# Two channel tiles of the gated convolution computed in token tiles and transposed back, in a four-layer float32 block on one core

## The chip, the core and the metric

The kernel runs on one NeuronCore of a Trainium2 chip. The engines are TensorE (PE: matmuls; its weight loads are PEld), VectorE (DVE), ScalarE (ACT), GpSimd (POOL) and the DMA queue that SyncE (SP) issues. The metric is the device time of one execution in microseconds (us), as the median of the runs shown.

## The reference, cut to what matters

A sequence of 512 tokens with 1024 channels passes four layers, each of them a mixer, a layer norm, a SwiGLU feed-forward and a layer norm. The change lies at the opening of the third layer's mixer:

```python
def short_gated_conv(p_a, conv_w):          # p_a = [B gate | C gate | value], 512 channels each
    return b_gate * causal_dwconv(c_gate * val, conv_w)      # 3 taps along the tokens

def multiscale_pool(u, w_grp, scale):       # u: 512 channels in 4 groups, windows 2, 4, 8, 16
    pooled = trailing_mean(u, window) - u   # along the tokens, each channel by itself
    return einsum("bsgc,gcd->bsgd", pooled, w_grp) * scale

def even_mixer(x, w_in, conv_w, pool_w, pool_scale, w_out):
    p = x @ w_in                            # 1024 -> b, c, v, u of 512 channels each
    return concat([short_gated_conv(b, c, v), multiscale_pool(u)]) @ w_out
```

In front of it stand the second layer's feed-forward (`ffn1`) and its layer norm.

## The kernel before, in words

Every float32 product is made of three matmuls: the weight is split into `whi` (its rounded high part) and `wlo` (the rest), the activation likewise (`XH`, `XL`), and hi·hi, hi·lo and lo·hi are summed in a PSUM bank. Weights come in units, 128x2048 values or so, into a ring of three places (`raw`, `whi`, `wlo`). For each unit in turn SP loads `raw`, ACT writes `whi` (`split_w`, L447), POOL writes `wlo` (`split_w`, L788) and PE uses it: `begin_unit` (L909) waits for `lo_ready`, that is for POOL, and the first matmul of a unit hands the unit before it back (`w_used`), upon which ACT may overwrite its place. ACT and POOL do all their work in one fixed order, written out by hand, so that a split of weights can stand behind a split of activations and the other way round.

**Layouts.** A channel tile is 128 channels x 512 tokens in one bank: the weight is stationary and all 512 tokens move through, so its first matmul needs all tokens. A token tile is 128 tokens x 512 channels: the tokens are stationary, and each of the four token tiles needs only its own tokens.

**The seam in question.** The feed-forward ends with token tiles t = 0 to 3 (`last_units`). DVE normalises tile t (`token_norm`) while PE computes t+1; PE transposes the normalised tile (`token_transposes`, eight 128x128 transposes), ACT copies it to `XH` and DVE writes `XL`. The last tile is transposed when its norm is done. Into the third layer PE then goes with `opening(2)` (L953): the first two channel tiles of u, which need all 512 tokens. Into the second layer it goes with `early_units` (L1112) instead: two units as four token tiles of 512 columns; the parts for t = 0 and 1 stand before the transposes of t = 3, those for t = 2 and 3 behind them.

**The third mixer's order.** The six units `ev_in` 0 to 5 hold two channel tiles each: u0 u1, u2 u3, then c and v of channel tile 0, 1, 2, 3. Behind them PE computes the four pooling products (`ev_pool`, from `EPH` and `EPL`) and four tiles of b. DVE works through four pooling tiles (copy of u, 1 to 4 doubling adds, the mean, two 16-column edge operations: L1953 to L1963, result `EP`) and then four convolution tiles (copy of c, product with v, three taps: L1614, L1968 to L1973, result `EY`). ACT's order is: the `whi` of `ev_in` 1 to 4, the four `EPH`, the `whi` of `ev_in` 5, `ev_pool`, `ev_b` 0 and 1. POOL's order is the same with `wlo` and `EPL`. (`ev_in` 0 has been split within the feed-forward.)

Of the kernel before, what the change touches and what calls it, by code (L numbers as in the profile page):

```python
# [26 lines left out]
F32 = mybir.dt.float32  # L27
F32R = mybir.dt.float32r
ALU = mybir.AluOpType
ACT = mybir.ActivationFunctionType  # L30

P = 128
S = 512
NB = S // P
D = 1024
KD = D // P
# [5 lines left out]
HALF = 512  # L42
# [123 lines left out]
def build(nc, x, xT, par, con, rcon, gb, w, out):  # L166
    ctx = ExitStack()
    with ctx:
        def sb(name, shape, dt=F32, stack=ctx):
            return stack.enter_context(nc.sbuf_tensor(name, shape, dt))  # L170

        def sem(name):
            return ctx.enter_context(nc.semaphore(name))
# [19 lines left out]
        idle = ExitStack()  # L193
# [4 lines left out]
        idle = ExitStack()  # L198
        fPT1 = sb("fPT1", [P, NB, S], F32, idle)
        idle.close()  # L200
        idle = ExitStack()
        mPT1 = sb("mPT1", [P, NB, S], F32, idle)
        idle.close()
        idle = ExitStack()
# [16 lines left out]
        ident = cons[:, CCOL["ident"]:CCOL["ident"] + P]  # L221
# [58 lines left out]
        EY = sb("EY", [P, KD, S], F32, ph)  # L280
        ec = shift
        EP = sb("EP", [P, 4, S], F32, ph)
        EPH = sb("EPH", [P, 4, S], F32R, ph)
        EPL = sb("EPL", [P, 4, S], F32R, ph)
        EAH = sb("EAH", [P, 4, S], F32R, ph)
        EAL = sb("EAL", [P, 4, S], F32R, ph)
        ez = sb("ez", [P, 2 + S], F32, ph)
# [20 lines left out]
        idle = ExitStack()  # L308
# [75 lines left out]
        gt_done = sem("gt_done")  # L384
        gt_free = sem("gt_free")
        cum_ready = sem("cum_ready")
        mem_ready = sem("mem_ready")
        small_dve = sem("small_dve")
        small_act = sem("small_act")
# [54 lines left out]
        def _(act):  # L444
            unit, tiles, srcs, auxf, gates, small = (Count() for _ in range(6))

            def split_w(n=1):  # L447

                for _ in range(n):
                    name, i, size, off, overlaps = UNITS[unit.n]  # L450
                    arrivals = unit.n // SEMS + (1 if unit.n % SEMS else 0)
                    act.wait_ge(raw_ready[unit.n % SEMS], 16 * arrivals)
                    if overlaps >= 0:
                        act.wait_ge(w_used, overlaps + 1)
                    act.copy(whi[:, off:off + size], raw[:, off:off + size]).then_inc(hi_ready, 1)  # L455
                    unit.add()
# [16 lines left out]
            def layer_norm(banks, early):  # L473

                for t in range(NB):
                    if t == 3 and early:
                        split_w()
                    for d in range(2):
                        act.wait_ge(xt_done, halves.at(1))
                        act.copy(XH[:, 4 * d:4 * d + 4, t * P:(t + 1) * P],  # L480
                                 bank[banks[(2 * t + d) % 4]][:].rearrange("p (k q) -> p k q", q=P)).then_inc(xh_ready, 1)
                        halves.add()
# [154 lines left out]
            split_w(2)  # L637
            layer_norm((0, 1, 2, 3), True)
            ffn()
            layer_norm((4, 5, 6, 7), False)  # L640


            split_w(4)
            for j in range(4):
                split_x(EPH[:, j, :], EP[:, j, :])
            tiles.add(12)
# [138 lines left out]
        def _(pool):  # L785
            unit, his, whis = Count(), Count(), Count()

            def split_w(n=1):  # L788

                for _ in range(n):  # L790
                    name, i, size, off, overlaps = UNITS[unit.n]
                    pool.wait_ge(hi_ready, whis.at(1))
                    pool.tensor_tensor(wlo[:, off:off + size], raw[:, off:off + size],  # L793
                                       whi[:, off:off + size].bitcast(F32), ALU.subtract).then_inc(lo_ready, 1)
                    unit.add()
                    whis.add()
# [21 lines left out]
            def layer_norm():  # L818

                for t in range(NB):  # L820
                    norms.add()
                    pool.wait_ge(tvar_ready, norms.at())
                    pool.tensor_tensor(troot[:, t:t + 1], tvar[:, t:t + 1], neg_half[:, 0:1], ALU.pow).then_inc(troot_ready, 1)  # L823
# [49 lines left out]
            layer_norm()  # L873
            ffn()
            layer_norm()
            split_w(4)
            for j in range(4):
                split_x(EPL[:, j, :], EP[:, j, :], EPH[:, j, :])
# [25 lines left out]
        def _(pe):  # L904
# [42 lines left out]
            def unit_tiles(nt, b0):  # L947

                off = begin_unit()
                for t in range(nt):  # L950
                    tile((b0 + t) % 4, [off + (k * nt + t) * P for k in range(KD)])

            def opening(nt, ks=range(KD)):  # L953

                off = begin_unit() - ks[0] * nt * P

                def lhs(wt, k, t):
                    return wt[:, off + (k * nt + t) * P:off + (k * nt + t + 1) * P]

                for k in ks:  # L960
                    if k % 4 == 0:
                        pe.wait_ge(xh_ready, norms.at(k // 4 - 1))
                    for which in (whi, wlo):
                        for t in range(nt):
                            if k == 0 and which is whi:
                                claim(t)
                            release(pe.matmul(bank[t][:], lhs(which, k, t), XH[:, k, :], start=k == 0 and which is whi, stop=False))  # L967
                for k in ks:
                    if k % 4 == 0:
                        pe.wait_ge(xl_ready, norms.at(k // 4 - 1))  # L970
                    for t in range(nt):
                        ins = pe.matmul(bank[t][:], lhs(whi, k, t), XL[:, k, :], start=False, stop=k == KD - 1)
                        if k == KD - 1:
                            tile_end(ins, t)
# [243 lines left out]
            def ffn(values=False):  # L1218
                for half in range(2):
                    n, first = HID[half], 0 if half else 2  # L1220
                    for j in range(first, n):
                        unit_tiles(2, 2 * (j % 2))
                        if half == 0 and j == 2:
                            early_transposes()
                    if first:
                        pe.wait_ge(early_lo, earlies.at())
                    ends = list(itertools.accumulate(DOWN[half], initial=0))
                    groups = [range(a, b) for a, b in zip(ends, ends[1:])]
                    for ks in groups:
                        first_steps(begin_unit(), ks, hidden, ks[0], n, 4, first)  # L1230
                    los.add(n - first)
                    tb0[0] = 4
                    last_units(groups, hidden, n, 0, half == 1, values)
# [208 lines left out]

            out_pair(OUT_KS, headed, (squares_of_head, spread_of_head, lambda: diff_out(7)))
            los.add(KD)
            ffn()


            opening(2)
            unit_tiles(2, 2)
            for i in range(4):  # L1450
                unit_tiles(2, 2 * (i % 2))
            off = begin_unit()
            for i in range(4):
                pe.wait_ge(act_lo, los.at(i + 1))
# [135 lines left out]
        def _(dve):  # L1590
# [4 lines left out]
            def link(ins):  # L1595

                ins.then_inc(step, 1)
                steps.add()
                dve.wait_ge(step, steps.at())
# [347 lines left out]
            def conv_col(k, i):  # L1947
                return pcol("conv_w", 4 * k + i)

            for i in range(4):  # L1950
                if i:
                    dve.wait_ge(src_ready, pooled + i)
                take(lambda: dve.tensor_copy(eu[0][:, PADW:], bank[i][:]))  # L1953
                dve.wait_ge(tile_free, tiles.at())
                src = eu[0]
                for d in range(i + 1):
                    dst = eu[1 + d % 2]
                    link(dve.tensor_tensor(dst[:, PADW:], src[:, PADW:], src[:, PADW - 2 ** d:PADW - 2 ** d + S], ALU.add))
                    src = dst

                link(dve.scalar_tensor_tensor(EP[:, i, PADW:], src[:, 2 * PADW:], 1.0 / WINDOWS[i], eu[0][:, 2 * PADW:], ALU.mult, ALU.subtract))
                link(dve.tensor_tensor(EP[:, i, 0:PADW], src[:, PADW:2 * PADW], cons[:, CCOL["invcnt"] + 16 * i:CCOL["invcnt"] + 16 * i + 16], ALU.mult))
                dve.tensor_tensor(EP[:, i, 0:PADW], EP[:, i, 0:PADW], eu[0][:, PADW:2 * PADW], ALU.subtract).then_inc(src_ready, 1)  # L1963
            for i in range(4):
                b = 2 * i % 4
                copy_tile(ec[:], b)
                dve.wait_ge(tile_free, tiles.at())
                take(lambda: dve.tensor_tensor(ez[:, 2:2 + S], bank[b + 1][:], ec[:], ALU.mult))  # L1968
                dve.wait_ge(tile_free, tiles.at())
                y = EY[:, i, :]  # L1970
                link(dve.tensor_scalar(y, ez[:, 0:S], conv_col(0, i), None, ALU.mult))
                for k in (1, 2):
                    link(dve.scalar_tensor_tensor(y, ez[:, k:k + S], conv_col(k, i), y, ALU.mult, ALU.add))  # L1973
            los.add(4)
            for i in range(4):
                take(lambda: dve.tensor_scalar(EY[:, 4 + i, :], bank[i][:], pcol("pool_s", i), None, ALU.mult))
# [136 lines left out]
def host_layout(inp):  # L2113
# [17 lines left out]
    w = {}  # L2131
# [30 lines left out]
    u, b = (win[:, :, i].reshape(KD, P, 2, 2, P).transpose(2, 1, 0, 3, 4).reshape(2, P, 2048) for i in (3, 0))  # L2162
    cv = win[:, :, 1:3].transpose(3, 1, 0, 2, 4).reshape(4, P, 2048)
    pool = f(inp["ev_pool_w_2"])[0].transpose(1, 0, 2).reshape(P, 512)
    w["ev_in"] = np.concatenate([u, cv])
    w["ev_pool"], w["ev_b"] = pool[None], b
    m = f(inp["ev_w_out_2"])[0]
    w["ev_o"] = down(np.concatenate([m[D // 2:], m[:D // 2]]), (4, 4))
# [62 lines left out]
```

## Time and profile before

| | us |
|---|---|
| median of 3 runs | 2356.08 (2351.93 to 2356.32) |
| the profiled execution | 2355.84 |
| its span, first to last instruction | 2354.1 |
| mean granted TensorE clock | 0.991 of full speed |

Busy shares of the span: PE 97%, PEld 78%, POOL 44%, DVE 31%, ACT 30%. The span is some 1.7 us shorter than the execution's own time. Times of instructions are counted from the span's start. A bracket behind a row of the timeline tells how long the engine sat idle before it and what released it.

### The profile page before, as it was taken

How to read it: one execution, taken by the hardware profiler on the slowest of the kernel's cores; microseconds unless marked ns; L12 is line 12 of the kernel's file. 1: busy time of each engine (PE TensorE's matmuls, PEld its weight loads, DVE VectorE, ACT ScalarE, POOL GpSimd, SP SyncE). 2: the span in 40 equal slices, each digit the busy share in tenths (PEclk: the TensorE clock that was granted, in tenths of full speed). 3: DMA queues.
4: the chain of work that ended last, by engine and by line, in shares of the span. 5: the costliest groups of instructions: out<-in, count | busy, mean ns of one | idle time of the engine just before them, and what ended most of it. 6: DMA issues, size and time to landing. Idle time of an engine off the chain costs nothing.

```text
span 2354.1 us, 24657 instructions
## 1 busy us (share of the span) xinstructions
PE 2294.1 (97%) x10303; PEld 1840.5 (78%) x10303; DVE 721.4 (31%) x1373; ACT 706.0 (30%) x1001; POOL 1026.6 (44%) x351
## 2 busy tenths in 40 slices
PE   8999999999999999999999999999998999999998
PEld 6667888888776778888878888888876667888887
DVE  6535000004466440010066410000269535000003
ACT  2453321222343232222222232222252563322220
POOL 3124553554333345445445455445532224554543
PEclk9999999999999999999999999999999999999999
DMA  4213223222212132322232232322221112332221
GB/s 169 73 72 140 93 90 107 90 75 81 99 50 90 36 125 90 107 90 83 99 110 90 90 125 90 107 90 90 99 72 36 56 53 91 124 99 98 90 90 54
DMA packets 32366, 212.60 MB, mean 90 GB/s; under 512 B 3584, under 2 KB 4736, under 8 KB 8832
## 3 DMA queue, kind: packets, MB, share of 16 engines
q1 hardware_dynamic: 32256, 211.03, 25.8%
q8 instruction: 82, 1.34, 0.2%
q14 instruction: 28, 0.23, 0.0%
HBM read 208.92 MB, written 2.10 MB: 90 GB/s over the span
## 4 chain that ended last, share of the span: by engine, by line
PE 88%; DVE 8%; ACT 2%; issue 1%; POOL 0%; DMA 0%; SPq 0%; DVEq 0%; ACTq 0%
PE bank L936 16%; PE bank L938 16%; PE bank L937 16%; PE bank L986 9%; PE bank L988 9%; PE bank L987 9%; DVE bank L2003 3%; PE bank L1047 2%; PE bank L1122 2%; PE bank L1123 2%; PE bank L1127 2%; PE bank L1165 1%; PE bank L1420 1%; PE bank L967 1%; PE bank L1025 1%
## 5 line engine op out<-in xcount | busy, mean ns | idle before, releaser
L793 POOL TENSOR_TENSOR wlo<-raw,whi 128x2048 fp32r<-128x2048 f32 (+5 forms) x184 | 842.8, 4582 | 670.7 <-ACT whi L455 662.4
L936 PE MATMUL bank<-XH,whi 128*128 128x512 f32 x1752 | 692.8, 395 | 9.3 <-POOL wlo L849 6.0
L938 PE MATMUL bank<-XH,wlo 128*128 128x512 f32 x1752 | 684.7, 391 | 0.0
L937 PE MATMUL bank<-XL,whi 128*128 128x512 f32 x1752 | 684.3, 391 | 0.0
L455 ACT CAST whi<-raw 128x2048 fp32r<-128x2048 f32 (+5 forms) x184 | 349.5, 1900 | 418.0 <-PE bank L986 304.5
L936 PEld LDWEIGHTS bank<-XH,whi 128*128 128x128 f32 x1752 | 330.4, 189 | 94.6 <-issue 19.0
L938 PEld LDWEIGHTS bank<-XH,wlo 128*128 128x128 f32 x1752 | 330.3, 189 | 70.0
L937 PEld LDWEIGHTS bank<-XL,whi 128*128 128x128 f32 x1752 | 330.6, 189 | 66.4
L1702 DVE TENSOR_TENSOR hf<-sil,bank 128x512 f32<-128x512 f32 x80 | 55.0, 688 | 814.4 <-PE bank L938 814.4
L986 PE MATMUL bank<-whi,HH 128*128 128x512 f32 x704 | 274.4, 390 | 0.0
L988 PE MATMUL bank<-wlo,HH 128*128 128x512 f32 x704 | 274.0, 389 | 0.0
L987 PE MATMUL bank<-whi,HL 128*128 128x512 f32 x704 | 273.9, 389 | 0.0
L807 POOL TENSOR_TENSOR HL<-hf,HH 128x512 fp32r<-128x512 f32 x80 | 103.6, 1295 | 376.3 <-ACT HH L503 376.3
L503 ACT CAST HH<-hf 128x512 fp32r<-128x512 f32 x80 | 49.6, 620 | 453.1 <-DVE hf L1702 453.1
L988 PEld LDWEIGHTS bank<-wlo,HH 128*128 128x128 f32 x704 | 132.1, 188 | 27.5
L987 PEld LDWEIGHTS bank<-whi,HL 128*128 128x128 f32 x704 | 132.2, 188 | 27.4
L986 PEld LDWEIGHTS bank<-whi,HH 128*128 128x128 f32 x704 | 132.1, 188 | 27.1
L1642 DVE SCALAR_TENSOR_TENSOR X<-X,bank 128x512 f32<-128x512 f32 x64 | 43.9, 687 | 279.4 <-PE bank L988 278.9
L499 ACT ACTIVATE sil<-bank 128x512 f32<-128x512 f32 x80 | 47.9, 598 | 186.2 <-PE bank L938 186.2
L823 POOL TENSOR_TENSOR troot<-tvar,neg_half 128x1 f32<-128x1 f32 x32 | 25.3, 791 | 129.8 <-DVE tvar L1668 129.8
L480 ACT CAST XH<-bank 128x512 fp32r<-128x512 f32 x56 | 30.7, 589 | 156.0 <-PE bank L1165 155.7
L2003 DVE SCALAR_TENSOR_TENSOR bank<-fz,parm,bank 128x512 f32<-128x512 f32 x90 | 68.0, 755 | 3.1
(273 smaller groups left out, 2254.1 us busy)
## 6 DMA issues: line engine op xcount, KB each, us to landing
raw<-w_ffn_gu SPq DMA_DIRECT2D x88, 1024.0 KB, 4.8
raw<-w_ffn_dn SPq DMA_DIRECT2D x40, 1024.0 KB, 4.8
GB<-gb SPq DMA_DIRECT2D x8, 1024.0 KB, 6.8
raw<-w_diff_in SPq DMA_DIRECT2D x6, 1280.0 KB, 5.7
raw<-w_ev_in SPq DMA_DIRECT2D x6, 1024.0 KB, 4.9
raw<-w_od_in SPq DMA_DIRECT2D x4, 1536.0 KB, 6.4
raw<-w_mla_pair SPq DMA_DIRECT2D x4, 1088.0 KB, 5.8
raw<-w_mla_o SPq DMA_DIRECT2D x4, 1024.0 KB, 6.0
```

Of the source, the lines that this page charges most:

```text
L455: act.copy(whi[:, off:off + size], raw[:, off:off + size]).then_inc(hi_ready, 1)
L503: act.copy(HH[:, j, :], hf[i][:]).then_inc(act_hi, 1)
L793: pool.tensor_tensor(wlo[:, off:off + size], raw[:, off:off + size], whi[:, off:off + size].bitcast(F32), ALU.subtract).then_inc(lo_ready, 1)
L807: pool.tensor_tensor(dst, src, hi.bitcast(F32), ALU.subtract).then_inc(act_lo, 1)
L936: release(pe.matmul(out, whi[:, off:off + P], xh, start=start, stop=False))
L937: pe.matmul(out, whi[:, off:off + P], xl, start=False, stop=False)
L938: return pe.matmul(out, wlo[:, off:off + P], xh, start=False, stop=stop)
L986: release(pe.matmul(bank[b][:], xh[:, rows], whi[:, off:off + HALF], start=start, stop=False))
L987: pe.matmul(bank[b][:], xl[:, rows], whi[:, off:off + HALF], start=False, stop=False)
L988: ins = pe.matmul(bank[b][:], xh[:, rows], wlo[:, off:off + HALF], start=False, stop=stop)
L1702: take(lambda: dve.tensor_tensor(hf[i][:], sil[i][:], bank[2 * i + 1][:], ALU.mult), 2)
L2003: ins = dve.scalar_tensor_tensor(acc, fz[i][:, k:k + S], wk, acc, ALU.mult, ALU.add)
```

## The change

The two first units of the mixer become c and v of channel tiles 0 and 1 (256 columns of c, 256 of v), computed as four token tiles by `early_units(0)`. ACT copies c of each token tile to SBUF (`ect`), DVE multiplies it with v from the bank (`ezt`). Then comes the unit of u0 and u1; between the two PE transposes `ezt` back into two banks of 128 channels x 512 tokens (eight 128x128 transposes), and DVE copies these to `ez` for the taps. After them come u2 u3, c and v of tile 2, c and v of tile 3. Within the last feed-forward's norm ACT splits `ev_in` 1 before the copies of the last token tile. POOL gets a wait for the whole norm before it splits `ev_in` 1. DVE's order becomes pooling 0, convolution 0, pooling 1, convolution 1, pooling 2, pooling 3, convolution 2, convolution 3. ACT and POOL keep all four `EPH` and `EPL` between `ev_in` 4 and `ev_in` 5.

```diff
@@ buffers (they lie over EAH, which is written later)
+        ect = sb("ect", [P, NB, 2 * P], F32, idle)
+        ezt = sb("ezt", [P, NB, 2 * P], F32, idle)
@@ ACT
-            layer_norm((4, 5, 6, 7), False)
-            split_w(4)
+            layer_norm((4, 5, 6, 7), True)
+            split_w()
+            for t in range(NB):
+                act.wait_ge(tile_done, tiles.at(t + 1))
+                act.copy(ect[:, t, :], bank[t][:, 0:2 * P]).then_inc(ec_ready, 1)
+            split_w(2)
             for j in range(4):
                 split_x(EPH[:, j, :], EP[:, j, :])
@@ POOL
             layer_norm()
+            pool.wait_ge(xn_ready, 2 * norms.n)
             split_w(4)
@@ PE
-            ffn()
-            opening(2)
+            ffn(True)
+            off = begin_unit()
+            tile(0, [off + 2 * k * P for k in range(KD)])
+            pe.wait_ge(tile_free, tiles.at(-1))
+            for e in range(2):
+                claim(4 + e)
+                for t in range(NB):
+                    ins = pe.transpose(bank[4 + e][:, t * P:(t + 1) * P], ezt[:, t, e * P:(e + 1) * P], ident)
+                ins.then_inc(zt_done, 1)
+                freed[4 + e] = (zt_free, e + 1)
+            tile(1, [off + (2 * k + 1) * P for k in range(KD)])
             unit_tiles(2, 2)
-            for i in range(4):
-                unit_tiles(2, 2 * (i % 2))
+            unit_tiles(2, 0)
+            unit_tiles(2, 2)
@@ DVE
+            for t in range(NB):
+                dve.wait_ge(ec_ready, t + 1)
+                take(lambda: dve.tensor_tensor(ezt[:, t, :], bank[t][:, 2 * P:4 * P], ect[:, t, :], ALU.mult))
             for i in range(4):
+                pool_tile(i)
+                if i < 2:
+                    dve.wait_ge(zt_done, i + 1)
+                    dve.tensor_copy(ez[:, 2:2 + S], bank[4 + i][:]).then_inc(zt_free, 1)
+                    dve.wait_ge(zt_free, i + 1)
+                    conv_tile(i)
+            for i in (2, 3):
                 (copy of c, product with v, conv_tile(i), as before)
@@ host
-    w["ev_in"] = np.concatenate([u, cv])
+    early = win[:, :, 1:3, 0:2].reshape(2, 4, P, HALF).transpose(0, 2, 1, 3).reshape(2, P, 2048)
+    w["ev_in"] = np.concatenate([early, u, cv[2:]])
```

## Rows read from the trace of the kernel before

**Rows 1.** The page's part 1: busy time of TensorE and its share of the span.

```profile
PE 2294.1 (97%) x10303; PEld 1840.5 (78%) x10303; DVE 721.4 (31%) x1373; ACT 706.0 (30%) x1001; POOL 1026.6 (44%) x351
```

**Rows 2.** Waits between 1195 and 1400 us: engine, line waited for, total, times, longest.

```profile
PE bank L1165 <- DVE X L1681: 3.0, 1, 3.0
...
PE bank L936 <- DVE EY L1976: 1.1, 1, 1.1
```

**Rows 3.** Timeline of PE at the seam: start, duration, instruction, idle time before it.

```profile
1208.16 1.04 PE L1165 MATMUL bank<-cons,X 128*128 128x128 f32 x8
1212.25 1.32 PE L1165 MATMUL bank<-cons,X 128*128 128x128 f32 x8 [3.05 <-DVE X L1681]
1213.78 1.19 PE L967 MATMUL bank<-XH,whi 128*128 128x512 f32 x2 [0.21 <-ACT XH L480]
```

**Rows 4.** Stretches: length, busy (count) by engine, granted clock; behind the stall, and second layer.

```profile
1213.78:1217.26 3.48, 3.48 (x9) 2.76 (x10) 1.55 (x7) 3.04 (x3) 0.65 (x1) 0.51 0.00 0
...
575.80:599.37 23.57, 23.57 (x113) 19.72 (x112) 9.65 (x17) 6.38 (x7) 10.21 (x3) 1.00 0.32 112
```

**Rows 5.** Timeline of PE: first matmuls of `ev_in` 2 and `ev_in` 5.

```profile
1237.23 0.39 PE L936 MATMUL bank<-XH,whi 128*128 128x512 f32 x1
...
1269.87 0.39 PE L936 MATMUL bank<-XH,whi 128*128 128x512 f32 x1
```

**Rows 6.** The chain that ended last: one set of eight transposes, early in feed-forward one.

```profile
246.66 0.87 PE bank L1148 x8
```

**Rows 7.** One line's instructions: DVE products of 128x256 from a bank, min/median/max ns.

```profile
L1694 DVE TENSOR_TENSOR hft<-silt,bank x16: 420/422/422, 228.8 to 2009.4; 128x256 f32<-128x256 f32 x16
```

**Rows 8.** Second layer's seam: POOL's second split there, and DVE's last token tile copy.

```profile
585.57 4.60 POOL L793 TENSOR_TENSOR wlo<-raw,whi 128x2048 fp32r<-128x2048 f32 x1 [0.53 <-ACT whi L455]
...
599.41 0.69 DVE L1614 COPY dVS<-bank 128x512 f32<-128x512 f32 x1 [2.03 <-PE bank L1127]
```

**Rows 9.** Timeline of DVE through the pooling and convolution tiles.

```profile
1226.32 0.69 DVE L1953 COPY eu<-bank 128x512 f32<-128x512 f32 x1 [10.99 <-PE bank L972]
...
1228.91 0.69 DVE L1953 COPY eu<-bank 128x512 f32<-128x512 f32 x1
1229.63 5.07 DVE L1958 TENSOR_TENSOR eu<-eu 128x512 f32<-128x512 f32 x2
...
1236.59 2.15 DVE L1958 TENSOR_TENSOR eu<-eu 128x512 f32<-128x512 f32 x3
...
1240.62 9.36 DVE L1958 TENSOR_TENSOR eu<-eu 128x512 f32<-128x512 f32 x4
...
1250.94 0.18 DVE L1963 TENSOR_TENSOR EP<-EP,eu 128x16 f32<-128x16 f32 x1
...
1252.48 0.95 DVE L1971 TENSOR_SCALAR EY<-ez,parm 128x512 f32<-128x512 f32 x1
...
1270.14 0.69 DVE L1968 TENSOR_TENSOR ez<-bank,shift 128x512 f32<-128x512 f32 x1 [4.75 <-PE bank L938]
...
1271.39 1.54 DVE L1973 SCALAR_TENSOR_TENSOR EY<-ez,parm,EY 128x512 f32<-128x512 f32 x2
```

**Rows 10.** Timeline of ACT: the `whi` of `ev_in` 5, behind the last `EPH`.

```profile
1251.67 1.91 ACT L455 CAST whi<-raw 128x2048 fp32r<-128x2048 f32 x1
```

**Rows 11.** Timeline of POOL: `wlo` of `ev_in` 3, three `EPL`, and `wlo` of `ev_in` 5.

```profile
1228.82 4.60 POOL L793 TENSOR_TENSOR wlo<-raw,whi 128x2048 fp32r<-128x2048 f32 x1 [3.04 <-ACT whi L455]
...
1244.30 5.14 POOL L807 TENSOR_TENSOR EPL<-EP,EPH 128x512 fp32r<-128x512 f32 x3
...
1251.85 1.30 POOL L807 TENSOR_TENSOR EPL<-EP,EPH 128x512 fp32r<-128x512 f32 x1 [2.41 <-ACT EPH L461]
1253.66 5.01 POOL L793 TENSOR_TENSOR wlo<-raw,whi 128x2048 fp32r<-128x2048 f32 x1 [0.52 <-ACT whi L455]
```

**Rows 12.** PE behind its longest wait, in the fourth layer: timeline rows.

```profile
1825.30 0.80 PE L1552 MATMUL bank<-fK,fQ 64*128 64x128 f32 x4 [8.31 <-DVE fK L1614]
...
1826.79 0.78 PE L936 MATMUL bank<-XH,whi 128*128 128x512 f32 x1
```

**Rows 13.** The same place as stretches (columns as in rows 4).

```profile
1830.00:1831.00 1.00, 1.00 (x4) 0.81 (x3) 0.93 (x2) 0.00 (x0) 0.00 (x0) 0.50 0.00 0
1831.00:1832.00 1.00, 1.00 (x4) 0.79 (x4) 0.00 (x0) 0.00 (x0) 0.00 (x0) 0.72 0.00 0
```

More of the change, by code:

```diff
@@ L284, in build @@
         EPL = sb("EPL", [P, 4, S], F32R, ph)
+        idle = ExitStack()
+        ect = sb("ect", [P, NB, 2 * P], F32, idle)
+        ezt = sb("ezt", [P, NB, 2 * P], F32, idle)
+        idle.close()
         EAH = sb("EAH", [P, 4, S], F32R, ph)
@@ L386, in build @@
         cum_ready = sem("cum_ready")
+        ec_ready = sem("ec_ready")
+        zt_done = sem("zt_done")
+        zt_free = sem("zt_free")
         mem_ready = sem("mem_ready")
@@ L1948, in conv_col, with pool_tile @@
                 return pcol("conv_w", 4 * k + i)
-            for i in range(4):
+            def pool_tile(i):
                 if i:
@@ L1963, in _, with conv_tile @@
                 dve.tensor_tensor(EP[:, i, 0:PADW], EP[:, i, 0:PADW], eu[0][:, PADW:2 * PADW], ALU.subtract).then_inc(src_ready, 1)
-            for i in range(4):
+            def conv_tile(i):
+                y = EY[:, i, :]
+                link(dve.tensor_scalar(y, ez[:, 0:S], conv_col(0, i), None, ALU.mult))
+                for k in (1, 2):
+                    link(dve.scalar_tensor_tensor(y, ez[:, k:k + S], conv_col(k, i), y, ALU.mult, ALU.add))
+            for t in range(NB):
+                dve.wait_ge(ec_ready, t + 1)
+                take(lambda: dve.tensor_tensor(ezt[:, t, :], bank[t][:, 2 * P:4 * P], ect[:, t, :], ALU.mult))
+            for i in range(4):
+                pool_tile(i)
[5 more added lines that the diff above has]
+            for i in (2, 3):
                 b = 2 * i % 4
@@ L1969, in _ @@
                 dve.wait_ge(tile_free, tiles.at())
[L1970 to L1973, printed above, removed]
+                conv_tile(i)
             los.add(4)
```

## The prediction

> **What bounds the kernel now.** I read the page first: PE is busy for 97% of the span [rows 1], so nearly every microsecond that PE does not stand still counts, and the work of DVE, ACT and POOL counts only where PE waits for it. Next I read the waits around the third mixer: PE waits there 3.0 us for the last token tile's norm and 1.1 us for a bank that DVE frees late [rows 2]. Then the timeline of PE at the seam. The reader should see three things: the transposes of token tile 2 at 1208.16, an idle time of 3.05 us before those of tile 3, and `opening` only from 1213.78 on, beginning slowly [rows 3]. The stretch behind it shows why: 3.48 us at a granted clock of 0.51, the lower of the two levels, 1.2 GHz instead of 2.4 [rows 4], after PE had stood still. Last I read DVE, ACT and POOL through the mixer, since the change puts their work into another order [rows 9 to 11].
>
> **Part 1: the seam itself, a gain.** From the transposes of tile 2 (1208.16) to the first matmul of the third unit, `ev_in` 2 (1237.23), PE now takes 29.07 us [rows 3, 5] for two sets of eight transposes and two units. The same work in the form that the change gives it stands in the trace already, at the second layer's seam: 23.57 us at full clock with no idle time [rows 4]. Gain: 29.07 - 23.57 = 5.50 us, made of the wait, the wait for `XH`, and the matmuls at half clock. The third mixer's units have the same size as those there, and the same number of instructions. So PE reaches `ev_in` 2 at 1208.16 + 23.57 = 1231.73.
>
> **Part 2: what is added on PE.** Eight transposes of `ezt`, 0.87 us for such a set [rows 6]. Their wait: the last product of DVE ends at about 1232.6 (in the second layer DVE gets the last token tile 0.04 us after PE has gone on [rows 4, 8]; here ACT's copy of 128x256 comes first, some 0.4 us by DVE's row for the same size, and then DVE's 0.42 us [rows 7]). PE asks for it only after tile u0, 5.44 us later (half a unit; `ev_in` 2, 3 and 4 take 1269.87 - 1237.23 = 32.64 us, 10.88 us each [rows 5]). Cost of the wait: nothing; u0 covers it, with 4.5 us to spare.
>
> Next, the splits at the seam. POOL's new wait for the norm puts `ev_in` 1 where the second layer's seam has it, and that seam runs without a gap [rows 4]; its second split there starts 9.77 us behind 575.80 [rows 8], so `wlo` of `ev_in` 2 ends at 1208.16 + 9.77 + 4.60 = 1222.5, against a use at 1231.73. Cost: nothing. But the `whi` of `ev_in` 3 and 4 now stand behind ACT's four copies of c, the last of which can't be made before 1231.8. With 1.91 us for `whi` [rows 10] and 4.60 us for `wlo` [rows 11], POOL writes `ev_in` 3 from 1234.0 to 1238.6, and `ev_in` 4 to 1243.6. PE wants them at 1231.73 + 10.88 + 0.87 = 1243.5 and 1254.4. Cost: nothing, with 4.9 us to spare at the nearer one.
>
> If nothing else happened, PE would reach `ev_in` 5 at 1254.37 + 10.88 = 1265.24, 4.63 us before the present 1269.87 [rows 5]. That is all that the change can gain.
>
> **Part 3: the split of `ev_in` 5, a loss.** PE's wait at `begin_unit` is for POOL's `wlo` of `ev_in` 5. In POOL's order it stands behind all four `EPL`, and in ACT's its `whi` stands behind all four `EPH`; both wait for DVE's fourth pooling tile. Today that tile is ready at 1251.12 and the `wlo` at 1253.66 + 5.01 = 1258.67, 7.55 us later [rows 9, 11], which leaves 11.2 us before its use at 1269.87 [rows 5]. In the new order u comes a unit and more later on PE, the use comes earlier, and DVE puts two convolution tiles between the pooling tiles.
>
> DVE's own work, uncontended: pooling tile 0 takes 1228.91 - 1226.32 = 2.59 us, each further add 0.72 us (2.15 us for three), so the four take 2.59 + 3.31 + 4.03 + 4.75 = 14.68 us; a convolution tile with its copy from the bank takes 1271.39 + 1.54 - 1270.14 = 2.79 us, two of them 5.58 us [rows 9]. It starts when u0 is complete, 1231.73 + 5.44 = 1237.2, and would end at 1257.5. The last pooling tile can't start before u3 is complete at 1254.37, so the least is 1254.4 + 4.75 = 1259.1.
>
> DVE is not uncontended. While POOL splits from 1228.82 for 4.60 us, two adds that should take 1.44 us take 5.07 us, and four adds beside a split and three `EPL` take 9.36 us in place of 2.9 [rows 9, 11]: an operation of DVE with both inputs in SBUF stands still until POOL's instruction ends, while its copies from a bank go on. In the new order POOL's splits of `ev_in` 3 and 4 (1234.0 to 1243.6) and three `EPL` fall into DVE's chain. The first add waits for the first split, ending at 1239.2 rather than 1238.6: 0.6 us. Pooling tile 0's mean then waits for the second split, until 1243.6, ending at 1244.2 rather than 1239.9: 4.3 us. Each `EPL` of 1.30 us [rows 11] holds up the operations of the tile behind it by 0.6 us if its start meets a copy or an operation that is first, 1.3 us at most; I take 0.9, three times 2.7 us. The fourth pooling tile is then ready at 1257.5 + 0.6 + 4.3 + 2.7 = 1265.1, and `wlo` of `ev_in` 5 7.55 us later, at 1272.65. PE stands still from 1265.24 on, for 7.4 us.
>
> The order of the two engines decides the size of that last term. The Trainium skill (SBUF — State Buffer, section Who interferes with whom) says that the engine that issues first has the shared port pair for its whole instruction, and that a `tensor_scalar` in a two-port mode contends as well; the first tap's 0.95 us beside an `EPL` speaks for it [rows 9, 11]. By that rule, with DVE first each time, the wait for the `EPL` would be the low 0.6 us three times and the sum below 0.9 us smaller.
>
> **Part 4: the clock.** A stop of 3.05 us cost 3.48 us at half speed, 1.7 us lost [rows 3, 4]. A stop of 8.31 us left PE at half speed from 1825.30 to about 1831.6, of which the full stream of matmuls from 1826.79 on has 4.8 us, so 2.4 to 3.1 us lost [rows 12, 13]. For 7.4 us I take 2.4, near the longer stop, with 1.7 and 3.1 as bounds.
>
> The Trainium skill (TensorE: Matmul & The Clock Gate, section What's actually happening) says not to fit such a ramp, since it is under one per cent of a usual span. Here it is 0.1% of the span and half of the result; by that advice the sum would be 2.4 us smaller.
>
> Behind `ev_in` 5 the distances are today's: `ev_pool` and `ev_b` are released by the start of `ev_in` 5 and of what follows it, and the 1.1 us wait for DVE [rows 2] stays, since the last c, v and pooling products stand as before. From there on PE is full and passes the shift on.
>
> **The sum.** `ev_in` 5 starts at 1272.65 in place of 1269.87, +2.8 us, and the clock adds 2.4: +5.2 us. The profiled execution took 2355.84 us, so 2361.0; the median of the runs is 0.24 above it, so 2361.3.
>
> **Rivals.** (a) The forecast: late split and clock loss. With the bounds for the `EPL` (1.8 to 3.9 us) and the clock (1.7 to 3.1) it reaches from +3.6 to +7.1, 2359.7 to 2363.2. (b) The split is late, but the clock stays up or loses under 1 us: +1.5 to +3.7, 2357.6 to 2359.8. Against it: both stops in rows 3 and 12 lost clock. (c) The other side, not slower. POOL's instructions don't meet DVE's: for instance because DVE gets in between the splits cheaply, or because the first split is over before u0 is. Then the fourth pooling tile is ready at 1259.1, the `wlo` at 1266.7, PE waits 1.4 us, too short for the clock to fall: 1266.7 - 1269.87 = -3.2 us, 2352.9. The result is not slower as long as DVE's delays by POOL sum to under 4.8 us (the 1.6 us that the wait for u3 hides, and 3.2), or under 2.4 us if the clock falls too, in place of my 7.6. Against it: 3.6 us and 6.5 us lost to POOL in two places today [rows 9]. (d) The change does not do what it says: POOL's new wait keeps `wlo` of `ev_in` 1 back and PE waits at the seam again. It is needed at 1220.8, and the second layer's seam has no such gap [rows 4]; it would add up to 3 us to (a), 2364.
>
> **How the numbers follow.** (a) 0.58, (b) 0.17, (c) 0.13, (d) 0.04, something unforeseen 0.08. A measurement of this kernel can tell about 0.2% from no change, 4.7 us: slower begins at 2360.8. Within (a) two thirds to three quarters lie above it, and (d) does: slower 0.48. Faster would need more than the 4.63 us of part 2, so only scatter of the runs (2351.93 to 2356.32) or a surprise gives it: 0.07. Same: 0.45. The range takes in (a), (b), the middle of (c) and its scatter: 2352.8 to 2363.8. (a)'s own range is 2359.7 to 2363.2.
>
> **What the profile after would show.** Right: no wait of PE at L1165 in the seam, 23.6 us from the transposes of tile 2 to `ev_in` 2, and one new wait of PE for POOL's `wlo` of about 7 us some 57 us behind the seam's start, with about 4 us at a clock near 0.5 after it; DVE's adds there several times as long as 0.7 us. Wrong: DVE's fourth pooling tile ready within 51 us of the seam's start (part 3's contention), the clock at 1.00 behind the wait (part 4), or a wait of PE at `ev_in` 3, `ev_in` 1 or the `ezt` transposes (part 2).

## The result, and the profile after

| | before | changed |
|---|---|---|
| median of 11 runs, us | 2356.25 (2351.93 to 2358.74) | 2360.75 (2358.11 to 2363.86) |
| the profiled execution, us | 2355.84 | 2360.99 |
| its span, us | 2354.1 | 2359.2 |
| ratio to before | | 1.0025, 95% interval 1.0017 to 1.0033 |

The changed kernel is 4.5 us slower, and the interval of the ratio excludes 1. The forecast was 2361.3 us. The prediction had put the least difference that can be told at 4.7 us, with slower and same nearly even (0.48 and 0.45); the measured time lies 0.05 us below that line.

PE's waits in the stretch that the change touches, 1195 to 1400 us, beside [rows 2] of before. Columns: line waited for, us in total, times, longest.

```profile
PE bank L948 <- POOL wlo L804: 7.2, 1, 7.2
...
PE bank L948 <- DVE EY L2013: 1.1, 1, 1.1
```

The wait of 3.0 us for the norm is gone and one of 7.2 us for POOL's `wlo` has come; the old 1.1 us is as it was. In the timeline of PE (start, duration, instruction, idle time before it), beside [rows 3] and [rows 5]:

```profile
1208.96 1.04 PE L1177 MATMUL bank<-cons,X 128*128 128x128 f32 x8
...
1232.53 0.39 PE L948 MATMUL bank<-XH,whi 128*128 128x512 f32 x1
...
1237.98 1.04 PE L1466 MATMUL bank<-cons,ezt 128*128 128x128 f32 x8
...
1273.47 0.80 PE L948 MATMUL bank<-XH,whi 128*128 128x512 f32 x1 [7.21 <-POOL wlo L804]
1274.06 0.63 PE L949 MATMUL bank<-XL,whi 128*128 128x512 f32 x1
...
1291.19 0.47 PE L948 MATMUL bank<-XH,whi 128*128 128x512 f32 x1 [1.11 <-DVE EY L2013]
```

From the transposes of token tile 2 (1208.96) to `ev_in` 2 (1232.53) PE takes 23.57 us where it took 29.07. The transposes of `ezt` begin right behind u0. Then `ev_in` 5 waits 7.21 us, and its matmuls start 0.43 us apart in place of 0.23. The stretches show the clock (length, busy and count of PE, PEld, DVE, ACT, POOL, granted clock, DMA share, GB/s):

```profile
1208.96:1232.53 23.57, 23.57 (x113) 19.73 (x112) 8.24 (x19) 6.88 (x9) 10.20 (x3) 1.00 0.37 135
1273.47:1279.40 5.93, 5.93 (x14) 4.69 (x15) 0.49 (x1) 1.90 (x1) 4.70 (x2) 0.51 0.84 297
```

Fourteen matmuls took 5.93 us behind the stop; at 0.227 us each (10.88 us for the 48 of a unit) they take 3.17: 2.8 us lost.

Why the `wlo` is late stands in DVE's timeline, beside [rows 9]:

```profile
1238.91 1.24 DVE L1980 TENSOR_TENSOR eu<-eu 128x512 f32<-128x512 f32 x1
1240.18 4.96 DVE L1983 SCALAR_TENSOR_TENSOR EP<-eu 128x496 f32<-128x496 f32 x1
...
1246.72 2.44 DVE L1992 SCALAR_TENSOR_TENSOR EY<-ez,parm,EY 128x512 f32<-128x512 f32 x2
...
1253.63 2.45 DVE L1992 SCALAR_TENSOR_TENSOR EY<-ez,parm,EY 128x512 f32<-128x512 f32 x2
...
1260.88 3.99 DVE L1980 TENSOR_TENSOR eu<-eu 128x512 f32<-128x512 f32 x4
...
1265.82 0.17 DVE L1985 TENSOR_TENSOR EP<-EP,eu 128x16 f32<-128x16 f32 x1
```

and in POOL's, beside [rows 11]:

```profile
1234.99 9.62 POOL L804 TENSOR_TENSOR wlo<-raw,whi 128x2048 fp32r<-128x2048 f32 x2 [11.47 <-ACT whi L462]
1246.29 1.54 POOL L818 TENSOR_TENSOR EPL<-EP,EPH 128x512 fp32r<-128x512 f32 x1 [1.68 <-ACT EPH L468]
...
1268.52 6.58 POOL L804 TENSOR_TENSOR wlo<-raw,whi 128x2048 fp32r<-128x2048 f32 x2 [0.53 <-ACT whi L462]
```

A mean that takes 0.68 us by itself took 4.96: it began while POOL was at its two splits and ended 0.5 us behind them. The pairs of taps took 2.4 us instead of 1.54 beside an `EPL`, the four adds 3.99 instead of 2.9.

**A finer measure.** Single runs of the kernel before lie up to 7.7 us apart, and their mean granted clock goes with the time: of its 81 runs beside the experiments, those with a clock of 0.994 took 2351 to 2352 us, those with 0.990 2357 to 2359. The experiments are therefore also told by a stretch of their traces, from the transposes of token tile 2 to the first matmul of the b tiles: 1284.74 - 1208.16 = 76.58 us before, 1291.19 - 1208.96 = 82.23 us changed, +5.65. The profiled executions as wholes differ by 5.1: the part ahead of the stretch took 0.8 us more in the changed one, the part behind it 1.35 us less, and no edit lies in either. The clock differs there too: from 1920 to 1930 us it is 0.83 in the trace before, which is 1.7 us lost, and 1.00 in the changed one. So part of what the times of two kernels differ by is such falls elsewhere.

### The profile page after: what moved, and what is told of

Same layout as the page of the kernel before. It is cut to its first block, busy times and chain, and to the rows that moved or that the text cites. A ratio compares the mean times of both kernels' runs of the same rounds, so it can differ in the third digit from the quotient of the medians.

```text
span 2359.2 us, 24684 instructions
## 1 busy us (share of the span) xinstructions
PE 2291.5 (97%) x10311; PEld 1839.2 (78%) x10311; DVE 718.3 (30%) x1375; ACT 707.1 (30%) x1005; POOL 1026.3 (44%) x351
## 4 chain that ended last, share of the span: by engine, by line
PE 86%; DVE 9%; ACT 2%; issue 1%; POOL 1%; DMA 0%; SPq 0%; DVEq 0%; ACTq 0%
PE bank L948 16%; PE bank L950 16%; PE bank L949 15%; PE bank L998 9%; PE bank L1000 9%; PE bank L999 9%; DVE bank L2040 2%; PE bank L1059 2%; PE bank L1134 2%; PE bank L1139 2%; PE bank L1135 2%; PE bank L1177 1%; PE bank L1432 1%; POOL wlo L804 1%; PE bank L1037 1%
## 5 line engine op out<-in xcount | busy, mean ns | idle before, releaser
L1134 PE MATMUL bank<-whi,XH 128*128 128x512 f32 x192 | 75.8, 395 | 0.0
```

The lines of the kernel that those rows point to most:

```text
L1134: release(pe.matmul(out, XH[:, k, rows], whi[:, cols], start=k == 0, stop=False))
```

## Experiments

Each was run beside the kernel before on its chip; e1 to e4 share one set of its runs (median 2354.62), e5 to e7 another (2355.05), e8 to e11 a third (2356.07).

| run | what differs | stretch, us | to before | median | ratio to before (95%) |
|---|---|---|---|---|---|
| changed | | 82.23 | +5.65 | 2360.75 | 1.0025 (1.0017 to 1.0033) |
| e1 | `ev_in` 5 split earlier | 77.80 | +1.22 | 2356.16 | 1.0007 (0.9998 to 1.0016) |
| e2 | PE kept busy in its wait | 79.65 | +3.07 | 2357.72 | 1.0013 (1.0004 to 1.0022) |
| e3 | DVE: pooling tiles first | 76.00 | -0.58 | 2356.80 | 1.0003 (0.9990 to 1.0017) |
| e4 | POOL: `EPL` behind `ev_in` 5 | 77.79 | +1.21 | 2356.56 | 1.0007 (0.9998 to 1.0016) |
| e5 | DVE's operands from PSUM | 73.67 | -2.91 | 2351.66 | 0.9986 (0.9976 to 0.9995) |
| e6 | e5 and e1 | 72.28 | -4.30 | 2349.56 | 0.9979 (0.9970 to 0.9987) |
| e7 | e6, last taps later | 70.74 | -5.84 | 2348.48 | 0.9968 (0.9956 to 0.9981) |
| e8 | before, with e7's DVE edits | 73.74 | -2.84 | 2350.95 | 0.9985 (0.9976 to 0.9993) |
| e9 | no norm wait on POOL | 86.10 | +9.52 | 2362.59 | 1.0032 (1.0021 to 1.0044) |
| e10 | e7 again | 70.74 | -5.84 | 2349.68 | 0.9973 (0.9963 to 0.9983) |
| e11 | changed again | 82.43 | +5.85 | 2360.45 | 1.0014 (1.0006 to 1.0023) |

**e1: split `ev_in` 5 earlier.** On ACT, and in the same way on POOL with `EPL`:

```diff
             for j in range(4):
+                if j == 2:
+                    split_w()
                 split_x(EPH[:, j, :], EP[:, j, :])
             tiles.add(12)
-            split_w(4)
+            split_w(3)
```

> The changed kernel, with one thing moved: ACT and POOL split ev_in 5 between the second and the third pooling tile (behind EPH/EPL 1, in front of EPH/EPL 2) and no longer behind all four. If the loss is the late split of ev_in 5, PE's wait of 7.2 us for POOL's wlo goes, and with it the stretch at half clock; what is left is the gain of the seam less the transposes, 5.50 - 0.87 = 4.6 us below the kernel before: 2351.6 us, ratio to before 0.998. Rival: the loss is in the token tiles themselves (their extra transposes, copies of c, products of 128x256): then the time stays near 2360.7.

The wait for `wlo` went, and the time did not fall as far as I had expected. PE's waits in e1, 1200 to 1300 us:

```profile
PE bank L952 <- DVE EY L2017: 5.0, 1, 5.0
PE bank L952 <- DVE shift L1639: 1.6, 1, 1.6
```

DVE now came late with the next things: the bank that its last copy of c frees (1.6 us), and the banks of the pooling products, whose scaled copies stand behind the last taps (5.0 us). The rows of DVE, and beside them those of POOL:

```profile
1251.10 6.68 DVE L1996 SCALAR_TENSOR_TENSOR EY<-ez,parm,EY 128x512 f32<-128x512 f32 x2
...
1270.04 6.67 DVE L1996 SCALAR_TENSOR_TENSOR EY<-ez,parm,EY 128x512 f32<-128x512 f32 x2
...
1278.20 3.53 DVE L1994 TENSOR_SCALAR EY<-ez,parm 128x512 f32<-128x512 f32 x1
```

```profile
1252.49 4.75 POOL L806 TENSOR_TENSOR wlo<-raw,whi 128x2048 fp32r<-128x2048 f32 x1 [0.26 <-ACT whi L462]
...
1269.68 6.49 POOL L806 TENSOR_TENSOR wlo<-raw,whi 128x512 fp32r<-128x512 f32 x2
...
1276.92 4.53 POOL L806 TENSOR_TENSOR wlo<-raw,whi 128x2048 fp32r<-128x2048 f32 x1 [0.75 <-ACT whi L462]
```

Two taps took 6.7 us instead of 1.54 twice over, and a first tap 3.53 instead of 0.49: DVE paid for the split of `ev_in` 5 at its new place too, and for both rows of splits behind it. So the order of POOL and ACT alone was not the cause; it had only decided which wait showed it. The clock fell behind the 5.0 us as well (0.59 over the 3.76 us from 1284.24 on, 1.5 us lost), which the stretch doesn't count, since it ends at 1284.24.

**e2: keep PE busy.** Right in front of `ev_in` 5:

```diff
             unit_tiles(2, 0)
+            off = UNITS[unit.n - 1][3]
+            for _ in range(28):
+                pe.matmul(bank[7][:], whi[:, off:off + P], XH[:, 0, :], start=True, stop=True)
             unit_tiles(2, 2)
```

> The changed kernel with 28 more matmuls of 512 columns (28 x 0.227 = 6.3 us at full clock) into a bank that nobody reads, right in front of PE's wait for ev_in 5; they use up most of the 7.2 us wait. They compute nothing of the output. If the clock falls because PE stands still there, it now stays at 1.00 behind the wait, the wait shrinks to about 0.9 us, ev_in 5 starts at the same time as in the changed kernel, and the time falls by what the half clock cost, 2.8 us: 2358.0. Rival: the half clock costs nothing that the end sees, or comes whatever PE does: 2360.7.

`ev_in` 5 began 64.64 us behind the transposes of tile 2 (1273.05 - 1208.41), against 64.51 in the changed kernel (1273.47 - 1208.96), and behind that the clock stayed up:

```profile
1273.05:1276.60 3.55, 3.55 (x16) 2.93 (x17) 0.49 (x1) 1.91 (x1) 2.62 (x2) 1.00 0.74 233
```

The stretch is 2.6 us shorter though PE computes 6.3 us more. That is the price of the half clock, with the wait left as it is.

**e3: pooling tiles first on DVE.**

```diff
             for i in range(4):
                 pool_tile(i)
+            for i in range(4):
                 if i < 2:
```

> The changed kernel with DVE's order changed alone: the four pooling tiles first, then the convolution tiles 0 and 1, then 2 and 3. My account: the two convolution tiles (2.8 us each and 0.9 us each lost to POOL) leave the chain to the fourth pooling tile, which is then bound by the arrival of u3: ready about 5 us after u3 is complete, so 5.5 to 6 us earlier than in the changed kernel; PE's wait for ev_in 5 shrinks from 7.2 to 1.3 to 2.3 us, the clock stays up: 2353 to 2354 us. Rival (DVE's chain is late through POOL's instructions alone, and its order doesn't matter): wait and time as in the changed kernel, 2360.7.

The fourth pooling tile was ready 52.1 us behind the transposes of tile 2 and not 57.0: 4.9 us earlier, where I had expected 5.5 to 6, since the last tile lost 0.85 us to an `EPL` (four adds in 3.72 us, 2.87 by themselves in e4). PE's wait was 2.1 us, within what I had expected. The clock did not stay up, as I had expected behind so short a stop:

```profile
1265.77:1269.50 3.73, 3.73 (x11) 2.96 (x12) 3.59 (x5) 1.90 (x1) 2.81 (x2) 0.63 0.72 242
```

Its ten runs fall in two groups, 2351.0 to 2353.2 and 2360.4 to 2362.5 us, with mean clocks of 0.993 to 0.994 and 0.991; the profiled one is of the first. What makes that gap of 8 us was not followed up, and the median, which stands between the groups, says little.

**e4: `EPL` behind `ev_in` 5 on POOL.**

```diff
             split_w(4)
             for j in range(4):
+                if j == 0:
+                    split_w()
                 split_x(EPL[:, j, :], EP[:, j, :], EPH[:, j, :])
-            split_w(4)
+            split_w(3)
```

> The changed kernel with POOL's order changed alone: wlo of ev_in 5 before the four EPL (ACT's order is as it was). The first three EPL no longer meet DVE's chain. If they cost DVE what the trace of the changed kernel shows (0.9, 0.9 and 1.1 us), the fourth pooling tile comes 2.9 us earlier, PE's wait falls from 7.2 to about 4.3 us, the clock still falls: 2357.4 to 2358.4. Rival: DVE's delays come from elsewhere and the chain stays: 2360.7.

The tile came 2.9 us earlier (1261.69 + 0.18 - 1207.78 = 54.1 us behind the transposes, against 57.0), the wait was 3.9 us. The three `EPL` cost DVE what their rows said. The stretch became 4.4 us shorter and not 2.9, and the median 2356.56 lies below the 2357.4 that I had as the least: from the tile to `ev_in` 5 it took 7.1 us and not 7.5, and the clock cost less behind the shorter stop (0.57 over 4.00 us, 1.7 us lost).

**e5: one operand of each DVE operation from PSUM.** All orders as in the changed kernel.

```diff
-                    link(dve.tensor_tensor(dst[:, PADW:], src[:, PADW:], src[:, PADW - 2 ** d:PADW - 2 ** d + S], ALU.add))
+                    link(dve.tensor_tensor(dst[:, PADW:], src[:, PADW:] if d else bank[i][:], src[:, PADW - 2 ** d:PADW - 2 ** d + S], ALU.add))
...
-                link(dve.scalar_tensor_tensor(EP[:, i, PADW:], src[:, 2 * PADW:], 1.0 / WINDOWS[i], eu[0][:, 2 * PADW:], ALU.mult, ALU.subtract))
+                link(dve.scalar_tensor_tensor(EP[:, i, PADW:], src[:, 2 * PADW:], 1.0 / WINDOWS[i], bank[i][:, PADW:], ALU.mult, ALU.subtract))
...
-                link(dve.tensor_scalar(y, ez[:, 0:S], conv_col(0, i), None, ALU.mult))
+                link(dve.tensor_scalar(y, z[:], conv_col(2, i), None, ALU.mult))
                 for k in (1, 2):
-                    link(dve.scalar_tensor_tensor(y, ez[:, k:k + S], conv_col(k, i), y, ALU.mult, ALU.add))
+                    ins = dve.scalar_tensor_tensor(y[:, k:], z[:, 0:S - k], conv_col(2 - k, i), y[:, k:], ALU.mult, ALU.add)
...
-                take(lambda: dve.tensor_tensor(ez[:, 2:2 + S], bank[b + 1][:], ec[:], ALU.mult))
+                take(lambda: dve.tensor_tensor(bank[4 + i][:], bank[b + 1][:], ec[:], ALU.mult))
```

Here z is the bank with the transposed product (tiles 0 and 1) or with DVE's own product (2 and 3); the copy to `ez` falls away, and the edge operations take the weights from a bank too. The bank of u is handed back at the end of its pooling tile and not behind the copy, and ACT waits for that in front of its `EPH`.

> The changed kernel in its own orders on all engines; only the operands of DVE's operations change: the taps read the product from a PSUM bank, a pooling tile's first add, mean and edges take one operand from u's bank or from a bank that holds the edge weights. So only the doubling adds after the first still read two SBUF inputs. Whole computation, same result. My theory, DVE's chain is late because operations with two SBUF inputs stand still beside POOL: the fourth pooling tile is then ready some 51.1 us behind the transposes of token tile 2 (57.0 in the changed kernel), PE's wait for ev_in 5 falls from 7.2 to about 1.5 us, the clock stays up, and the b tiles begin 73.6 us behind those transposes (82.2 changed, 76.6 before): 3 us under the kernel before, 2352 us beside 2355. Rival: the order and sheer amount of DVE's work make it late: three operations less per convolution tile save 1.2 us in two tiles, wait 6 us, time 3 us above before.

DVE's timeline in e5, beside a POOL that works through the same splits (9.20 us from 1234.43 on):

```profile
1238.34 0.69 DVE L1985 TENSOR_TENSOR eu<-bank,eu 128x512 f32<-128x512 f32 x1
1239.07 0.67 DVE L1988 SCALAR_TENSOR_TENSOR EP<-eu,bank 128x496 f32<-128x496 f32 x1
...
1240.84 1.53 DVE L1997 SCALAR_TENSOR_TENSOR EY<-bank,parm,EY 128x511 f32<-128x511 f32 x2
...
1259.43 0.17 DVE L1990 TENSOR_TENSOR EP<-EP,bank 128x16 f32<-128x16 f32 x1
```

```profile
1234.43 9.20 POOL L804 TENSOR_TENSOR wlo<-raw,whi 128x2048 fp32r<-128x2048 f32 x2 [11.50 <-ACT whi L462]
```

The mean that took 4.96 us takes 0.67 beside the same split, and POOL's pair of splits is shorter too, 9.20 against 9.62. The fourth pooling tile is ready 51.2 us behind the transposes, PE waits 1.1 us, the clock stays up. Only where an operation reads its inputs was changed, so the delay was that of two SBUF inputs beside POOL, and not the amount of DVE's work. (The edit also takes 1.1 us of work out of this chain, 20.1 to 19.0 us without delays. That isn't what brought the tile forward: DVE now stands idle 3.0 us for PE in the chain, and its fourth pooling tile begins when u3 is there.)

**e6: e5 with e1's earlier split.** No further edit.

> As e5, and the split of ev_in 5 behind the second EPH and EPL as in e1. In e1 PE's wait only moved to DVE's tiles (1.6 and 5.0 us), because POOL's splits then met DVE's taps. If that was the two engines' shared way to SBUF, then without it neither the wait for wlo nor those for DVE are left beyond the old 1.1 us: b tiles at 72.0 us behind the transposes of token tile 2, 4.6 us under before. Rival: DVE's own work does not fit, and a wait of 2 us or more at the pooling products or b tiles stays: no better than before.

```profile
PE bank L952 <- DVE EY L2025: 1.4, 1, 1.4
```

That is PE's only wait from 1195 to 1300 us. The same edit of POOL's and ACT's order that moved the wait in e1 now removes it.

**e7: the last taps later.**

```diff
                 take(lambda: dve.tensor_tensor(bank[4 + i][:], bank[b + 1][:], ec[:], ALU.mult))
                 dve.wait_ge(tile_free, tiles.at())
-                conv_tile(i, bank[4 + i])
+                if i == 2:
+                    conv_tile(i, bank[4 + i])
             los.add(4)
             for i in range(4):
                 take(lambda: dve.tensor_scalar(EY[:, 4 + i, :], bank[i][:], pcol("pool_s", i), None, ALU.mult))
+            conv_tile(3, bank[7])
```

> As e6, with the three taps of convolution tile 3 moved behind the four scaled copies of the pooling products on DVE. The old wait of 1.1 us of PE in front of the b tiles (for a bank that DVE frees) should go: b tiles at 70.9 us behind the transposes of token tile 2, 5.7 us under before. Rival: the wait has another cause than the taps in front of those copies and stays at 1.1 us.

No wait of PE is left in the stretch. e7 has only five runs. **e10** is this kernel again:

> The kernel of e7 a second time, beside e8 and the changed kernel on one chip: 6 to 6.6 us under before (ratio 0.997), 4.6 us under e8.

It is 6.4 us under before, as expected, and 1.3 us under e8, where I had expected 4.6: e8 came out too fast for that, as told next.

**e8: the kernel before with the DVE edits of e7.**

> The kernel before with DVE's operands from PSUM as in e5 and the taps of convolution tile 3 moved as in e7; no token tiles, no other order. It tells how much of e7's gain needs the change. My theory: the kernel before had 11 us in hand in front of ev_in 5, so the freed DVE time is worth nothing there and only the 1.1 us wait in front of the b tiles goes: seam stretch 75.5 us (76.6 before), time 1 us under before, and e7 is 4.6 us faster than this. Rival: most of e7's gain comes from DVE's operands alone, and this one is 4 us or more faster than before.

This expectation failed: the stretch is 73.74 us and not 75.5, and the median is 5.1 us under before, where I had expected 1 and the rival 4 or more. The stop of 3.05 us at the seam is there, and so is the wait for `XH`, but in this execution the clock did not fall behind them. Compare the first of [rows 4], same place and length, 0.51:

```profile
1212.47:1215.95 3.48, 3.48 (x15) 2.89 (x16) 1.73 (x8) 3.33 (x3) 0.93 (x1) 1.00 0.00 0
```

So 1.1 us is the tail, as expected, and 1.7 the clock, which DVE's operands can't have moved: nothing that they touch comes before that place. Outside the stretch e8's trace is another 2.7 us shorter than before's, 1.3 of them ahead of it, where no edit lies; there the clock was 0.96 and 0.86 in the two stretches of 10 us from 730 on before, and 1.00 in e8. But six of e8's eleven runs have a mean clock of 0.994 and two of before's 27, so this is not one odd execution; why e8's mean clock is higher is open, and so is how much of the 5.1 us the DVE edits earn. Between e8 and e7 lie 3.0 us in this pair of traces and 1.3 us in the medians of e8 and e10; the intervals of their ratios to before (0.9985 and 0.9973) overlap from 0.9976 to 0.9983.

**e9: the changed kernel without POOL's wait for the norm.**

```diff
             layer_norm()
-            pool.wait_ge(xn_ready, 2 * norms.n)
             split_w(4)
```

> The changed kernel without POOL's wait for the whole norm in front of the split of ev_in 1. POOL can then begin that split as soon as ACT's whi is there, about 1.2 us before the last norm operations of DVE have run. If POOL's instruction holds up DVE operations with two SBUF inputs, the last operation of the norm (both halves read X and the gain or shift row in SBUF) ends some 4 to 4.6 us later, the transposes of token tile 3 wait about 2 to 3 us for it, and the seam loses that much: the new wait for ev_in 5 starts later and is as long, or a little shorter, so 0 to 3 us above the changed kernel. Rival: the wait does nothing, the seam stays at 23.6 us and the time at that of the changed kernel.

```profile
1209.84 5.71 DVE L1701 SCALAR_TENSOR_TENSOR X<-X,troot,GB 128x512 f32<-128x512 f32 x2
```

```profile
1210.16 4.85 POOL L804 TENSOR_TENSOR wlo<-raw,whi 128x2048 fp32r<-128x2048 f32 x1 [0.49 <-ACT whi L462]
```

```profile
1215.61 0.96 PE L1176 MATMUL bank<-cons,X 128*128 128x128 f32 x4 [2.12 <-DVE X L1701]
```

The last pair of the norm took 5.71 us in place of 1.41, since POOL had begun 0.3 us behind its start. PE stood still for 2.1 us in the transposes of tile 3, and the clock fell behind it (0.50 in the 2.98 us from 1216.22 on): from the transposes of tile 2 to the first matmul of the third unit PE took 27.52 us in place of 23.57. I had allowed for the wait and not for the clock. The median is 2.1 us above that of e11, the changed kernel in the same set. The line `pool.wait_ge` is a needed part of the change.

**e11: the changed kernel again.**

> The changed kernel itself a second time, on this chip: its stretch from the transposes of token tile 2 to the b tiles was 5.65 us longer than before in the two traces; theory: 4.5 to 5.7 us above before again. Rival: the measured 4.5 us was scatter of the clock elsewhere, and it is nearer to 2 us.

Its stretch is 5.85 us over before's and PE's wait 7.3 us. The medians differ by 4.4 us, about as in the first set and just under the 4.5 expected, while the ratio of this set is 1.0014: within two sets the same two kernels stand 1.7 to 3.3 and 0.6 to 2.3 thousandths apart.

## Why the prediction was right

**Part 1, the seam** (5.50 us gained). Right: 23.57 us to the hundredth. But the 5.50 held a part that is not sure. e8 shows the same stop without the fall of the clock; the gain is then 3.8 us. I had taken the one trace's clock for the rule.

**Part 2, the additions.** Right in each point: the `ezt` transposes stood without a wait and cost 0.87 us (in e7, with no wait at all, `ev_in` 5 begins 57.14 us behind the transposes of tile 2, and by the sum 57.08), and `ev_in` 3 and 4 came in time. The last product of DVE ended at 1233.56, 1.0 us behind PE's entry into u0, against 0.9 reckoned.

**Part 3, the split of `ev_in` 5.** Right in cause and size. The fourth pooling tile was to be ready at 1265.1; it was at 1265.99, which is 1265.19 once the 0.8 us are taken off by which this execution ran late. Its terms: 0.6 us forecast for the first add, 0.55 measured (1.24 - 0.69); 4.3 us for the mean, 4.28 measured (4.96 - 0.68); three times 0.9 for the `EPL`, and 0.9, 0.9 and 1.1 measured. `wlo` was to be ready at 1272.65, and `ev_in` 5 began at 1273.47 - 0.8 = 1272.67.

The cause is shown and not only argued: e5 takes the second SBUF input away and leaves every order as it was, and the chain becomes 5.8 us shorter. e4 takes the three `EPL` away and gets their 2.9 us back; e3 takes the two convolution tiles out of the chain and gets 4.9 us, a little less than expected. The Trainium skill (SBUF — State Buffer, section Who interferes with whom) has the rule that e5 rests on: a DVE instruction with at most one SBUF input, outside the two-port modes, does not contend with GpSimd. The traces agree: 0.67 us beside a split that made it 4.96. The same section of the Trainium skill says that `tensor_scalar` can enter a two-port mode and contends then. In e1 it took 3.53 us in place of 0.49.

What part 3 did not say is that DVE had no room anywhere in the stretch. I had written that behind `ev_in` 5 the distances were today's, which was true only as long as the late `ev_in` 5 gave DVE the time. e1 took that wait away and met the next.

**Part 4, the clock** (2.4 us, bounds 1.7 and 3.1). Measured 2.8 in the trace and 2.6 by e2, inside the bounds. The Trainium skill (TensorE: Matmul & The Clock Gate, section What's actually happening) says that "the ramp penalty is <1% of a typical kernel span". A sum that left it out for that would have given 2358.9 and missed half of the effect. The rows I went by don't make a rule of the stop's length: I had taken both stops before for a sure loss and, for e3, one of 1.3 to 2.3 us for none, and the clock fell behind 2.1 us (e3, e9) and stayed up behind 3.05 us (e8). For the 1.4 us of rival (c) it held: behind 1.1 and 1.4 us in e5 it was 1.00.

**The sum.** +5.2 us forecast for the stretch, +5.65 and +5.85 in two traces, +4.5 and +4.4 between medians. The forecast of the time is so near the result in part by luck, since falls of the clock outside the stretch move single executions by more than the 0.55 us between the two. Rival (b), no clock loss, falls with e2; rival (c), little contention, with part 3's rows; rival (d), a wait at the seam because POOL's new wait holds back `wlo` of `ev_in` 1, with the 23.57 us without a wait. e9 shows the opposite: it is without POOL's wait that PE stands still there.

**A better version.** With the cause removed the change is worth making: e7 and e10 run at 0.9968 and 0.9973 of before, 6 to 7 us less, and beat both kernels. But without the token tiles the same DVE edits give 0.9985 (e8), 5.1 us less between medians: most of the 6.4 us is there without the change. What the token tiles add to it is 3.0 us between the traces and 1.3 us between the medians, and not shown clear of the scatter.

## What to carry to other kernels

When a change pulls a stage forward, list what has to be ready sooner because of it, and look for the item whose preparation stands behind the pulled stage's own results in another engine's fixed order. If a wait disappears and the time does not follow, read the next wait before the next idea: here one shared resource paid for each of them. And where DVE and GpSimd work at the same time, take one operand of DVE's from PSUM if it is there anyway; this made a 4.96 us operation one of 0.67 us without any change of order.

## What the runs showed of the hardware that was not expected

- A stop of PE of 2.1 us can bring its clock to half (0.50 over 2.98 us in e9), and one of 3.05 us with slower transposes behind it can leave it at 1.00 (e8), where the same place in the kernel before had 0.51.
- A `tensor_scalar` with one SBUF input and an SBUF output took 3.53 us instead of 0.49 beside a split of POOL (e1); from a bank it took 0.74 us beside a split and 0.75 beside none (e5). Where POOL is busy, the slower form is the faster one.
- GpSimd is held up as well: its pair of splits took 9.62 us beside DVE's two-input operations and 9.20 us without them (e5).
